# A 21-stage float32 kernel on one core: instruction orders changed in its second and fourth token mixers

## The chip, the cores and the metric

The kernel runs on one core of a Trainium2 chip. The metric is the device time of one execution in microseconds (us); lower is better. The engines are TensorE (PE, with its weight loads as PEld), VectorE (DVE), ScalarE (ACT), GpSimd (POOL) and SyncE (SP), which here issues the weight transfers. Each engine runs its own list of instructions strictly in order and meets the others only through semaphores.

## What is computed

The input is one sequence of 512 tokens with 1024 features, in float32. Two model blocks of two layers each follow one another: norms, token mixers and feed-forward parts. The change touches two of the mixers.

```
def odd_mixer(...):                       # the second mixer
    u, c_q, c_kv, k_rope = split_cols(h @ w_in, ODD_SIZES)
    y_c = s5_group(u, ...)                # linear state space scan, gelu, gate
    y_d = mla_group(c_q, c_kv, k_rope, pos, ...)   # 8 heads, causal by chunks of 64
    return concatenate([y_c, y_d]) @ w_out

# s5_group: A, B are complex, per group of 16 channels
    bu = einsum(u, b_bar); state = associative_scan(a, bu)
    y = real(einsum(state, c)) + d_skip * u
    y = gelu(y); y = y * sigmoid(y @ w_glu + b_glu)

# mla_group
    q = rms_norm(c_q, q_norm) @ w_uq; kv = rms_norm(c_kv, kv_norm) @ w_ukv
    o = softmax(mask((q . k) * scale)) @ v       # q and k each: 64 plain + 32 rotated features

def mlstm_mixer(x, ...):                  # 4 heads, forward and backward in time, chunks of 64
    h = mlstm(q, k, v, gates_forward) + flip(mlstm(flip(...), gates_backward))
    h = normalised over each head's 256 features * norm_g
    return (sigmoid(o) * h) @ w_out
```

## The kernel before, in words

The whole program is one launch of 21 stages. Weights come as 512 KB units of 128 x 1024 numbers, in one fixed order, into a ring of six buffers; SyncE loads unit n once unit n-6 is done on TensorE. Every float32 product is made from three fast products: ScalarE rounds a number to a high part (`hi_to` for the weights, tile WH), VectorE subtracts to get the low part (`lo_to`, tile WL), and TensorE adds high*high, low*high and high*low (lines L310 to L312). The activations have the same two parts, XH and XL. `hi_to(act, n)` and `lo_to(dve, n)` split all units below n, at the place of the program where they stand.

No scheduler orders anything: each mixer has one function per engine (`pe`, `act`, `dve`, `pool`), and the order of calls in it is the order on the engine. An engine that waits on a semaphore holds up all that stands behind it.

**The second mixer** (`od_mixer`; its tiles have names with od_). Units nu to nu+9 are the input projection, nuq to nuq+2 (nu+10 to nu+12) make the queries, nu+13 and nu+14 keys and values, ng and ng+1 the gate, no onward the output. The steps that matter below:

- The normed query and key inputs: VectorE makes `cn(q)` (od_cn, two buffers), ScalarE its high part (od_cqh, od_ckh), VectorE its low part (od_cql, od_ckl), five times.
- B and C of the state space are multiplied by powers of A on VectorE (`turned`, tiles od_bp and od_cp). ScalarE spreads each power into a plane (`plane(d)` writes od_bm, `c_planes(d)` writes od_cmr and od_cmi). TensorE transposes the planes of B into od_bt.
- VectorE rotates queries and keys (od_ab, od_qr, od_kr), with od_cos and od_sin, and builds a table of powers (od_tab).
- Four scans, one per 128 channels: TensorE `states_in(c)` (ps<-od_u,od_bt), VectorE `scan(c)` (od_t, od_vb, then the result in X[c], od_x), TensorE `states_out(c, part)` (ps<-od_u,od_kd, then od_x with od_cmr and od_cmi, and in part 1 od_u,od_skip). ScalarE takes the result (`y(c)`, od_u).
- Eight attention heads. Per head h: TensorE `scores(h)` (ps<-od_k,od_q, into banks 0 to 2), VectorE `maxes(h)`, ScalarE `exps(h)` (od_p), VectorE `weights(h)` (1/sum on a diagonal, od_dgr), TensorE the normalising transposes (ps<-od_dgr,od_p), ScalarE their copies (od_pt), TensorE the product with the values (ps<-od_pt,od_v), ScalarE and VectorE its parts XH and XL. I call the TensorE parts scores, turns and output of a head. Between them stand parts of gelu on ScalarE and VectorE, and on TensorE what the table `beside` names: `states_out` of scans 2 and 3, and the two gate units (ps<-od_gh,WH).

**The mLSTM mixer** (`mlstm_mixer`, tiles with ml_). For each of 4 heads, TensorE `values(h, j)` (ps<-ml_v,ml_e) for four tiles j of 128 tokens, then per tile VectorE `sums` (ml_rc, later ml_h) with ScalarE `backward` (ml_hb) in the middle, then `scales(h)` on VectorE and `normed(h)` on ScalarE; TensorE `turn(h, c)` transposes ml_h, VectorE `gated(k)` multiplies with ml_sig, ScalarE `high(k)` writes XH and VectorE `low(k)` writes XL, for eight k of 128 features. `output(m, ks)` adds the products of k in ks to output tile m; each m has its own unit and bank. `gate(t)` is the o-gate's unit t.

Of the kernel before, what the change touches and what calls it, by code (L numbers as in the profile page):

```python
# [11 lines left out]
P = 128  # L12
# [1867 lines left out]
def od_mixer(nc, b):  # L1880
# [48 lines left out]
    X = [sb("od_x0", [P, 4, 2, NC], at=WORK2 + 8 * KB), sb("od_x1", [P, 4, 2, NC], at=WORK2), sb("od_x2", [P, 4, 2, NC], at=WORK + 80 * KB)]  # L1929
    X += X[1:2]  # L1930
# [38 lines left out]
    GAN = counts("y0 y1 s0 t0 s1 t1 y2 s2 t2 y3 s3 t3 h0 h1 h2 h3 z0 z1 x0 x1 z2 z3 x2 x3")  # L1969
# [27 lines left out]
    def pe(pe, e):  # L1997
# [34 lines left out]
        for g in range(3):  # L2032
            if g == 0:
                pe.wait_ge(s["u_ev"], 3)
            elif g == 1:
                pe.wait_ge(s["u_ev"], 4)
                pe.wait_ge(s["c_ready"], 3)
            else:
                pe.wait_ge(s["q_ev"], 4)
# [11 lines left out]
            elif g == 1:  # L2051
                for a in range(2):
                    pe.wait_ge(s["q_ev"], a + 1)
                    mm(ps[:, a, :], perm[:], QR[:, a, :]).then_inc(s["rot"], 1)
# [84 lines left out]
        pe.wait_ge(s["k_ev"], 21)  # L2139
        states_out(1, 0)  # L2140
        states_out(1, 1)

# [13 lines left out]
        def gate(g):  # L2156
# [4 lines left out]
        beside = {0: lambda: states_out(2, 0), 1: lambda: states_out(2, 1), 2: lambda: states_out(3, 0), 3: lambda: states_out(3, 1),  # L2161
                  5: lambda: gate(0), 6: lambda: gate(1)}
        scores(0)
        for h in range(NH):
            pe.wait_ge(s["comb"], h + 1)
# [10 lines left out]
            if h + 1 < NH:  # L2176
                scores(h + 1)
# [16 lines left out]
    def act(act, own, e):  # L2194
# [49 lines left out]
        hi_to(act, nu + 14)  # L2244
# [107 lines left out]

        y(0)
        y(1)
        exps(0)
        for h in range(NH):
# [18 lines left out]
            if h in (1, 3):  # L2375
                y(2 + h // 2)
# [10 lines left out]
    def dve(dve, own, e, finish, tail):  # L2387
# [96 lines left out]

        own(turned(CP[1], CP[0], AR, XK, C1, C2), "c_ready")
# [23 lines left out]
        def scan(c):  # L2509
# [974 lines left out]
```

## Time and profile before

| | |
|---|---|
| median of 3 runs | 3600.67 us (3599.86 to 3603.81) |
| the profiled execution's own time | 3600.57 us |
| its span | 3598.8 us |
| TensorE busy | 3446.1 us (96%) |
| VectorE busy | 1856.8 us (52%) |
| ScalarE busy | 1309.2 us (36%) |
| transfers | 307.60 MB, mean 85 GB/s |
| mean granted TensorE clock | 0.983 of full |

"Busy" is the time in which an engine had an instruction running. The span runs from the first to the last instruction of the profiled execution. A matmul's start and its length overlap with its neighbours', so the distance from start to start is what one costs in a dense stretch. The granted clock is 1.00 at 2.4 GHz and 0.5 at 1.2 GHz; a mean over a stretch lies between.

### The profile page before, as it was taken

The page shows a single profiled execution, that of the slowest core. Times are in us where ns is not written, and L with a number is a line of the kernel's source. Part 1 is how long each engine was busy: PE and PEld are TensorE (multiplying, and loading weights), DVE is VectorE, ACT ScalarE, POOL GpSimd, SP SyncE. Part 2 cuts the span into 40 slices and gives each one's busy share as a digit, 9 for nine tenths or more (in the row PEclk, how much of TensorE's full clock was granted, in tenths as well). Part 3 has the DMA queues.
Part 4 walks back from the last instruction along what each step waited for, and adds up shares of the span by engine and source line. Part 5 has one row for each costly group of instructions (what it writes and reads, how often), then busy time and mean ns, then how long its engine had stood idle before and what let it go on. Part 6 is the DMA issues. An engine that isn't in the chain of part 4 may idle for free.

```text
span 3598.8 us, 43337 instructions
## 1 busy us (share of the span) xinstructions
PE 3446.1 (96%) x17564; PEld 2834.9 (79%) x17564; DVE 1856.8 (52%) x2971; ACT 1309.2 (36%) x2212; POOL 92.8 (3%) x133
## 2 busy tenths in 40 slices
PE   8989999999978999999999998999999999999998
PEld 7657778888855888888888767888888888788886
DVE  5665775433784544354435346543364336564446
ACT  4442433222454422243223343422242225543233
POOL 0000000000100000000001000100010001010000
PEclk9999999999988999999999999999999999999999
DMA  3102112233300222323232211222322232013244
GB/s 130 53 24 88 59 60 94 100 100 106 92 25 6 77 100 96 104 90 104 100 100 82 101 39 56 82 99 95 105 88 95 98 106 73 30 48 121 96 141 157
DMA packets 92507, 307.60 MB, mean 85 GB/s; under 512 B 16014, under 2 KB 17684, under 8 KB 92308
## 3 DMA queue, kind: packets, MB, share of 16 engines
q1 hardware_dynamic: 89528, 301.31, 25.1%
q10 hardware_dynamic: 2780, 3.51, 0.3%
q8 instruction: 140, 2.29, 0.3%
q14 instruction: 59, 0.48, 0.0%
HBM read 302.69 MB, written 2.10 MB: 85 GB/s over the span
## 4 chain that ended last, share of the span: by engine, by line
PE 81%; DVE 12%; ACT 4%; issue 2%; DMA 0%; SPq 0%; DVEq 0%; POOL 0%; ACTq 0%
PE ps L310 23%; PE ps L311 22%; PE ps L312 22%; PE ps L307 12%; DVE XT L853 1%; DVE WL L298 1%; ACT WH L292 1%; DVE mb_cv L1755 1%; DVE XL L859 1%; PE ps L2738 1%; ACT od_p L2330 0%; DVE R L700 0%; DVE small L2555 0%; DVE mb_e L1816 0%; DMA RAW<-units 0%
## 5 line engine op out<-in xcount | busy, mean ns | idle before, releaser
L310 PE MATMUL ps<-XH,WH 128*128 128x512 f32 (+1 forms) x3200 | 1190.3, 372 | 43.3 <-DVE XL L859 25.9
L311 PE MATMUL ps<-XL,WH 128*128 128x512 f32 (+1 forms) x3200 | 1174.2, 367 | 0.0
L312 PE MATMUL ps<-XH,WL 128*128 128x512 f32 (+1 forms) x3200 | 1173.7, 367 | 0.0
L298 DVE TENSOR_TENSOR WL<-RAW,WH 128x1024 fp32r<-128x1024 f32 x567 | 688.1, 1228 | 320.7 <-ACT WH L292 317.2
L310 PEld LDWEIGHTS ps<-XH,WH 128*128 128x128 f32 x3200 | 608.8, 190 | 153.8 <-DVE XL L859 19.1
L312 PEld LDWEIGHTS ps<-XH,WL 128*128 128x128 f32 x3200 | 609.0, 190 | 97.6
L311 PEld LDWEIGHTS ps<-XL,WH 128*128 128x128 f32 x3200 | 609.6, 190 | 96.1 <-issue 1.7
L292 ACT ACTIVATE WH<-RAW 128x1024 fp32r<-128x1024 f32 x567 | 586.7, 1049 | 138.9 <-DMA RAW<-units 73.6
L310 PE MATMUL ps<-HH,WH 128*128 128x512 f32 (+1 forms) x990 | 362.7, 366 | 0.0
L311 PE MATMUL ps<-HL,WH 128*128 128x512 f32 (+1 forms) x990 | 361.8, 365 | 0.0
L312 PE MATMUL ps<-HH,WL 128*128 128x512 f32 (+1 forms) x990 | 361.7, 365 | 0.0
L589 ACT ACTIVATE HH<-HV 128x512 fp32r<-128x512 f32 x132 | 83.4, 632 | 566.2 <-DVE HV L774 566.2
L771 DVE SCALAR_TENSOR_TENSOR SG<-TH,ps 128x512 f32<-128x512 f32 x132 | 90.7, 687 | 299.1 <-ACT TH L586 298.9
L774 DVE SCALAR_TENSOR_TENSOR HV<-SG,ps 128x512 f32<-128x512 f32 x132 | 90.7, 687 | 296.2 <-PE ps L312 296.0
L700 DVE SCALAR_TENSOR_TENSOR R<-R,ps 128x512 f32<-128x512 f32 (+1 forms) x86 | 51.6, 600 | 362.9 <-PE ps L312 362.2
L490 ACT ACTIVATE SQ<-R 128x512 f32<-128x512 f32 (+1 forms) x89 | 49.1, 551 | 514.2 <-DVE R L700 435.3
L586 ACT ACTIVATE TH<-ps 128x512 f32<-128x512 f32 x132 | 78.7, 596 | 368.5 <-PE ps L312 368.5
L310 PEld LDWEIGHTS ps<-HH,WH 128*128 128x128 f32 x990 | 186.7, 189 | 30.4
L312 PEld LDWEIGHTS ps<-HH,WL 128*128 128x128 f32 x990 | 186.7, 189 | 30.1
L311 PEld LDWEIGHTS ps<-HL,WH 128*128 128x128 f32 x990 | 186.7, 189 | 30.0
L776 DVE TENSOR_TENSOR HL<-HV,HH 128x512 fp32r<-128x512 f32 x132 | 91.5, 693 | 101.5 <-ACT HH L589 101.5
L549 POOL TENSOR_TENSOR XT<-XT,NB 128x256 f32<-128x256 f32 x80 | 74.8, 950 | 2115.0 <-DVE XT L853 2115.0
(607 smaller groups left out, 3467.4 us busy)
## 6 DMA issues: line engine op xcount, KB each, us to landing
RAW<-units SPq DMA_DIRECT2D x567, 512.0 KB, 3.3
XIN<-in_x ACTq DMA_DIRECT2D x2, 1024.0 KB, 6.4
out<-YT SPq DMA_DIRECT2D x8, 256.0 KB, 3.2
GB<-in_ln_g SPq DMA_DIRECT2D x1, 512.0 KB
GB<-in_ln_b SPq DMA_DIRECT2D x1, 512.0 KB
da_pi<-in_positions ACTq DMA_DIRECT2D x1, 256.0 KB, 3.0
mb_pairf<-constants ACTq DMA_DIRECT2D x1, 256.0 KB
wa_dist<-constants ACTq DMA_DIRECT2D x1, 192.0 KB, 2.3
```

Source lines behind the costliest of these rows:

```text
L292: nc.scalar.activation(WH[:, u % RING, :], RAW[:, u % RING, :], ACT.Copy).then_inc(S["wh_ready"], 1)
L298: nc.vector.tensor_tensor(WL[:, u % RING, :], RAW[:, u % RING, :], WH[:, u % RING, :].bitcast(F32), ALU.subtract)\
L307: return nc.tensor.matmul(out, lhsT, rhs, start=start, stop=stop, **kw)
L310: nc.tensor.matmul(out, wh, xh, start=start, stop=False)
L311: nc.tensor.matmul(out, wh, xl, start=False, stop=False)
L312: return nc.tensor.matmul(out, wl, xh, start=False, stop=stop)
L549: nc.gpsimd.tensor_tensor(x, x, NB[:, t // 8, :], ALU.add).then_inc(S["t_ready"], 1)
L586: nc.scalar.activation(TH[:, j % 2, :], ps[:, 2 * (j % 3), :], ACT.Tanh, scale=0.5).then_inc(S["ffn_act"], 1)
L589: nc.scalar.activation(HH[:, j, :], HV[:, j % 2, :], ACT.Copy).then_inc(S["ffn_act"], 1)
L771: own(v.scalar_tensor_tensor(SG[:, j % 2, :], TH[:, j % 2, :], 1.0, ps[:, b, :], ALU.add, ALU.mult))
L774: own(v.scalar_tensor_tensor(HV[:, j % 2, :], SG[:, j % 2, :], e["half"], ps[:, b + 1, :], ALU.mult, ALU.mult), "ffn_dve")
L776: own(v.tensor_tensor(HL[:, j, :], HV[:, j % 2, :], HH[:, j, :].bitcast(F32), ALU.subtract), "ffn_dve")
```

## The change

Nothing is computed in another way; the number of instructions of each kind stays the same, but for one activation more that only sets ScalarE's function table. What moves:

1. Second mixer, input side. ScalarE's copy `u(2)` and the splitting of unit nu+12 no longer stand ahead of the five high parts; `plane(0)` and `plane(1)` move ahead of the copies od_qr, `queries(1)` behind `plane(3)`, and the split of unit nu+13 behind it. VectorE makes the first power of C ahead of those of B, turns the key behind both powers of B, and splits unit nu+13 last. TensorE rotates the queries' source (od_qr,od_perm) ahead of unit nuq+1 and not behind it.
2. Scans. X[2] and X[3] get places of their own, and VectorE's two waits for a free place go (on bt_t 12 and on yc 2).
3. Heads. `scores(h+1)` stands ahead of head h's turns on TensorE, not behind them; `states_out` of scans 1 and 2 stands behind `scores(0)`, ahead of all turns, and scan 3's takes the places beside heads 0 and 1. ScalarE loads the table of exp ahead of `y(0)`, does `exps(0)` ahead of `y(1)`, and `exps(0)` waits for three scans, not four.
4. mLSTM. `values(3, 0)` and `values(3, 1)` stand ahead of gate unit 7, and `values(3, 2)` ahead of the second turn. On VectorE `sums(3, 0)` and `sums(3, 1)` come ahead of the first `low`. The first four output tiles are added up in slices of k (0 to 2, 3, then the turns of head 3, then 4 and 5, then 6 and 7), where before tile 0 and then tile 1 took k 0 to 5, and tiles 2 and 3 came last and whole.

```diff
-    X = [sb("od_x0", [P, 4, 2, NC], at=WORK2 + 8 * KB), sb("od_x1", [P, 4, 2, NC], at=WORK2), sb("od_x2", [P, 4, 2, NC], at=WORK + 80 * KB)]
-    X += X[1:2]
+    X = [sb("od_x0", [P, 4, 2, NC], at=WORK2 + 8 * KB), sb("od_x1", [P, 4, 2, NC], at=WORK2)]
+    X += [sb(f"od_x{c}", [P, 4, 2, NC], at=XH_AT + 4 * c * KB) for c in (2, 3)]
...
             elif g == 1:
+                for a in range(2):
+                    pe.wait_ge(s["q_ev"], a + 1)
+                    mm(ps[:, a, :], perm[:], QR[:, a, :]).then_inc(s["rot"], 1)
                 pe.wait_ge(s["u_ev"], 4)
...
-        pe.wait_ge(s["k_ev"], 21)
-        states_out(1, 0)
-        states_out(1, 1)
...
-        beside = {0: lambda: states_out(2, 0), 1: lambda: states_out(2, 1), 2: lambda: states_out(3, 0), 3: lambda: states_out(3, 1),
-                  5: lambda: gate(0), 6: lambda: gate(1)}
+        beside = {0: lambda: states_out(3, 0), 1: lambda: states_out(3, 1), 5: lambda: gate(0), 6: lambda: gate(1)}
         scores(0)
+        pe.wait_ge(s["k_ev"], 21)
+        for c in (1, 2):
+            states_out(c, 0)
+            states_out(c, 1)
         for h in range(NH):
+            if h + 1 < NH:
+                scores(h + 1)
             pe.wait_ge(s["comb"], h + 1)
...
-            if h + 1 < NH:
-                scores(h + 1)
             if h in beside:
...
-        for t in range(3):
+        for t in range(2):
             u(t)
             hi_to(act, nu + 11 + t)
         for q in range(5):
...
+            if q == 3:
+                u(2)
+        hi_to(act, nu + 13)
...
         def exps(h):
             act.wait_ge(s["max_ready"], h + 1)
-            if h == 0:
-                act.wait_ge(s["x"], 4)
-            if h >= 2:
+            if h < 2:
+                act.wait_ge(s["x"], 3 + h)
+            else:
                 act.wait_ge(s["tr"], 4 * (h - 1))
...
+        A(TMPA[:, 0:1], ones[:, 0:1], ACT.Exp)
         y(0)
+        exps(0)
         y(1)
-        exps(0)
+        y(2)
...
-            elif c == 2:
-                dve.wait_ge(s["bt_t"], 12)
-            elif c == 3:
-                dve.wait_ge(s["yc"], 2)
...
         pe.wait_ge(s["exp"], 56)
-        output(0, range(6))
-        output(1, range(6))
+        for m in range(4):
+            if m == 2:
+                pe.wait_ge(s["ho"], 15)
+            output(m, range(3))
+        for m in range(4):
+            output(m, (3,))
         turn(3, 0, "gy", 5)
         turn(3, 1, "gy", 6)
-        output(0, (6, 7))
-        output(1, (6, 7))
-        outproj_pe(pe, b, e, no, None, XHk, XLk, first=2)
+        for ks in ((4, 5), (6, 7)):
+            for m in range(4):
+                output(m, ks)
+        outproj_pe(pe, b, e, no, None, XHk, XLk, first=4)
```

ScalarE, input side of the second mixer, of before and then of the change (od_u is a copy of a projected tile, WH<-RAW the split of a weight unit, od_bm a plane of B):

```order
L2206 ACTIVATE od_u<-ps 128x512
L292 ACTIVATE WH<-RAW 128x1024
L2239 ACTIVATE od_cqh<-od_cn 128x512 x3
L2239 ACTIVATE od_ckh<-od_cn 128x512 x2
L2242 DMA od_q<-constants 4x8x512
L2206 ACTIVATE od_u<-ps 128x512
L292 ACTIVATE WH<-RAW 128x1024
L2283 ACTIVATE od_qr<-ps 128x512 x2
L2211 ACTIVATE od_bm<-od_bp_168,small 128x2x16x16 x2
```

```order
L2237 ACTIVATE od_cqh<-od_cn 128x512 x3
L2237 ACTIVATE od_ckh<-od_cn 128x512
L2204 ACTIVATE od_u<-ps 128x512
L2237 ACTIVATE od_ckh<-od_cn 128x512
L292 ACTIVATE WH<-RAW 128x1024
L2243 DMA od_q<-constants 4x8x512
L2204 ACTIVATE od_u<-ps 128x512
L2209 ACTIVATE od_bm<-od_bp_168,small 128x2x16x16 x2
L2209 ACTIVATE od_bm<-od_bp_169,small 128x2x16x16 x2
L2285 ACTIVATE od_qr<-ps 128x512 x2
```

The first row of before (the copy of the third tile, which waits for TensorE) and the split behind it now stand inside and behind the high parts, and two planes stand ahead of od_qr.

TensorE, heads 4 and 5 of the second mixer, of before and then of the change (od_dgr,od_p are a head's turns, od_k,od_q the next head's scores, od_pt,od_v its output):

```order
L307 MATMUL ps<-od_dgr,od_p_208 128x128 x10
L307 MATMUL ps<-od_k,od_q 128x512
L307 MATMUL ps<-od_k,od_q 128x128
L307 MATMUL ps<-od_k,od_q 128x384
L307 MATMUL ps<-od_k,od_q 128x256
L307 MATMUL ps<-od_pt_210,od_v 64x512
L307 MATMUL ps<-od_pt_210,od_v 64x384
L307 MATMUL ps<-od_pt_210,od_v 64x256
L307 MATMUL ps<-od_pt_210,od_v 64x128
L307 MATMUL ps<-od_dgr,od_p_209 128x128 x10
```

```order
L307 MATMUL ps<-od_k,od_q 128x512
L307 MATMUL ps<-od_k,od_q 128x128
L307 MATMUL ps<-od_k,od_q 128x384
L307 MATMUL ps<-od_k,od_q 128x256
L307 MATMUL ps<-od_dgr,od_p_209 128x128 x10
L307 MATMUL ps<-od_pt_211,od_v 64x512
L307 MATMUL ps<-od_pt_211,od_v 64x384
L307 MATMUL ps<-od_pt_211,od_v 64x256
L307 MATMUL ps<-od_pt_211,od_v 64x128
```

Scores of the next head have moved from behind a head's turns to ahead of them.

ScalarE, end of the mLSTM mixer, of before and then of the change (ml_hb is `backward`, ml_sig `gate(7)`, XH<-ml_sig `high`, ml_h `normed`):

```order
L3196 ACTIVATE ml_h<-ml_h,ml_tm 128x256 x4
L3167 ACTIVATE ml_sig<-ps 128x512
L292 ACTIVATE WH<-RAW 128x1024
L3201 ACTIVATE XH<-ml_sig,ml_gain 128x512
L3191 ACTIVATE ml_hb<-ps,ml_rc 128x256
L3201 ACTIVATE XH<-ml_sig,ml_gain 128x512
L3191 ACTIVATE ml_hb<-ps,ml_rc 128x256
L3201 ACTIVATE XH<-ml_sig,ml_gain 128x512
```

```order
L3200 ACTIVATE ml_h<-ml_h,ml_tm 128x256 x4
L292 ACTIVATE WH<-RAW 128x1024
L3195 ACTIVATE ml_hb<-ps,ml_rc 128x256 x2
L3170 ACTIVATE ml_sig<-ps 128x512
L3205 ACTIVATE XH<-ml_sig,ml_gain 128x512 x2
L3195 ACTIVATE ml_hb<-ps,ml_rc 128x256
L3205 ACTIVATE XH<-ml_sig,ml_gain 128x512
```

The first two `backward` of head 3 have moved ahead of the gate's activation and of the first two high parts.

## Rows read from the trace of the kernel before

**Rows 1.** Windows: stretch, us and count busy by engine, granted clock, DMA share, GB/s.
```profile
1020.00:1185.00 165.00, 125.55 (x948) 88.77 (x947) 92.67 (x165) 73.84 (x178) 1.80 (x1) 0.87 0.04 14
2166.00:2222.00 56.00, 46.00 (x183) 36.80 (x182) 31.25 (x82) 17.79 (x29) 0.00 (x0) 0.88 0.12 38
...
1146.75:1152.34 5.59, 5.59 (x26) 1.00 0.02 3
1165.17:1172.95 7.78, 7.78 (x24) 0.71 0.00 0
```

**Rows 2.** Timeline (start, length, [idle before <-releaser]), ScalarE then VectorE, input side.
```profile
975.75 0.60 ACT L2206 ACTIVATE od_u<-ps 128x512 f32<-128x512 f32 x1 [6.84 <-PE ps L312]
...
977.92 0.69 DVE L2462 TENSOR_TENSOR od_cql<-od_cn,od_cqh 128x512 fp32r<-128x512 f32 x1 [6.13 <-ACT od_cqh L2239]
```

**Rows 3.** Timeline, TensorE: third query unit starts; VectorE: the table starts.
```profile
993.15 0.79 PE L310 MATMUL ps<-od_cqh,WH 128*128 128x512 f32 x1
...
1001.29 0.07 DVE L2490 MEMSET od_tab<- 128x16 f32 x1
```

**Rows 4.** Timeline, TensorE: `states_in(1)` of the second scan.
```profile
1024.93 1.28 PE L307 MATMUL ps<-od_u,od_bt 32*128 32x128 f32 x16 [4.51 <-DVE od_t L2517]
```

**Rows 5.** Timeline, VectorE: results of scans 2 and 3.
```profile
1055.06 0.69 DVE L2532 TENSOR_TENSOR od_x<-od_vb,od_t 128x512 f32<-128x512 f32 x1 [1.45 <-PE ps L307]
...
1069.16 0.69 DVE L2532 TENSOR_TENSOR od_x<-od_vb,od_t 128x512 f32<-128x512 f32 x1 [4.03 <-PE ps L307]
```

**Rows 6.** Timeline, TensorE: `states_out(1)`, `scores(0)`, first turns.
```profile
1063.56 2.57 PE L307 MATMUL ps<-od_u,od_kd 128*128 128x512 f32 x8
...
1068.89 2.32 PE L307 MATMUL ps<-od_k,od_q 100*128 100x512 f32 x8
1077.78 1.44 PE L307 MATMUL ps<-od_dgr,od_p 128*128 128x128 f32 x5 [6.56 <-DVE od_dgr L2565]
```

**Rows 7.** Timeline, TensorE: turns and output of one head, and the next turns.
```profile
1126.01 2.90 PE L307 MATMUL ps<-od_dgr,od_p 128*128 128x128 f32 x20 [0.86 <-DVE od_dgr L2565]
...
1131.00 2.37 PE L307 MATMUL ps<-od_pt,od_v 128*64 128x512 f32 x8
1136.22 3.35 PE L307 MATMUL ps<-od_dgr,od_p 128*128 128x128 f32 x14 [2.85 <-DVE od_dgr L2565]
1142.36 1.01 PE L307 MATMUL ps<-od_dgr,od_p 128*128 128x128 f32 x3 [2.78 <-ACT od_pt L2361]
```

**Rows 8.** Timeline, VectorE, same head: maxima, last gelu step.
```profile
1131.11 1.68 DVE L2555 TENSOR_REDUCE small<-ps 128x1 f32<-128x512 f32 x4 [3.15 <-PE ps L307]
...
1138.91 0.69 DVE L2541 SCALAR_TENSOR_TENSOR od_u<-od_gw,od_u 128x512 f32<-128x512 f32 x1
```

**Rows 9.** Timeline, ScalarE: the gate's four high parts; TensorE: gate unit 1, last output.
```profile
1139.64 2.19 ACT L2380 ACTIVATE od_gh<-od_u 128x512 fp32r<-128x512 f32 x4 [0.93 <-DVE od_u L2541]
...
1165.17 0.79 PE L310 MATMUL ps<-od_gh,WH 128*128 128x512 f32 x1 [5.32 <-ACT od_y L2347]
...
1178.96 2.34 PE L307 MATMUL ps<-od_pt,od_v 128*64 128x512 f32 x8 [0.51 <-ACT od_pt L2361]
```

**Rows 10.** Timeline, TensorE, end of mLSTM: values of head 3 and output products.
```profile
2171.79 4.49 PE L307 MATMUL ps<-ml_v,ml_e 128*128 128x257 f32 x20
...
2179.36 6.29 PE L307 MATMUL ps<-ml_v,ml_e 128*128 128x257 f32 x20 [2.20 <-DVE ml_h L3302]
...
2194.37 0.80 PE L310 MATMUL ps<-XH,WH 128*128 128x512 f32 x1 [4.78 <-DVE XL L3318]
...
2202.78 1.04 PE L3056 MATMUL ps<-ident,ml_h 128*128 128x128 f32 x8
2205.95 0.47 PE L310 MATMUL ps<-XH,WH 128*128 128x512 f32 x1 [2.13 <-DVE XL L3318]
```

**Rows 11.** Timeline, VectorE: third XL part; output tile 3 taken.
```profile
2183.19 0.75 DVE L3318 SCALAR_TENSOR_TENSOR XL<-ml_sig,ml_gain,XH 128x512 fp32r<-128x512 f32 x1
...
2221.51 0.69 DVE L700 SCALAR_TENSOR_TENSOR R<-R,ps 128x512 f32<-128x512 f32 x1 [0.30 <-PE ps L312]
```

More of the change, by code:

```diff
@@ L1968, in od_mixer @@
     GLN = counts("w0 g0 w1 g1 w2 g2 w3 g3 l0 l1 l2 l3 m0 m1 x0 x1 m2 m3 x2 x3")
-    GAN = counts("y0 y1 s0 t0 s1 t1 y2 s2 t2 y3 s3 t3 h0 h1 h2 h3 z0 z1 x0 x1 z2 z3 x2 x3")
+    GAN = counts("y0 y1 y2 s0 t0 s1 t1 y3 s2 t2 s3 t3 h0 h1 h2 h3 z0 z1 x0 x1 z2 z3 x2 x3")
     N_ROW, N_IN = 5, 12
@@ L2050, in pe @@
                 last.then_inc(s["rot"], 1)
[L2051 to L2054, printed above, removed]
         for n in range(8):
@@ L2243, in act @@
         u(3)
-        hi_to(act, nu + 14)
         def queries(g):
@@ L2279, in keys @@
                 A(K[0:64, h, :], ps[0:64, PB[h % 4], :], ACT.Copy).then_inc(s["k_ev"], 1)
+        plane(0)
+        plane(1)
         act.wait_ge(S["unit_done"], done_at(e["nuq"]))
@@ L2283, in act @@
             A(QR[:, a, :], ps[:, a, :], ACT.Copy).then_inc(s["q_ev"], 1)
-        plane(0)
         act.wait_ge(s["rot"], 2)
@@ L2287, in act @@
         A(SIN[:], ps[:, 3, :], ACT.Copy).then_inc(s["q_ev"], 1)
-        plane(1)
-        queries(1)
         plane(2)
         plane(3)
+        queries(1)
+        hi_to(act, nu + 14)
         queries(2)
@@ L2374, in act @@
                 tanh(min(h, 3))
-            if h in (1, 3):
-                y(2 + h // 2)
+            if h == 1:
+                y(3)
             elif h == 4:
@@ L2468, in dve @@
             own(v.tensor_tensor(CP[0][:, i], CP[0][:, i], both[:, :, 1, :], ALU.add), "c_ready")
-        lo_to(dve, nu + 14)
+        own(turned(CP[1], CP[0], AR, XK, C1, C2), "c_ready")
         for d in range(2):
@@ L2472, in dve @@
             own(turned(BP[d], BP[1 - d], AR, XK, B1, B2), "b_ready")
-            if d == 0:
+            if d == 1:
                 dve.wait_ge(s["q_ev"], 4)
@@ L2483, in dve @@
             own(v.tensor_tensor(QR[:, a, :], AB[:, 0, :], AB[:, 1, :], ALU.add), "rope_done")
-        own(turned(CP[1], CP[0], AR, XK, C1, C2), "c_ready")
+        lo_to(dve, nu + 14)
         dve.wait_ge(s["ws"], 1)
@@ L3101, in pe @@
             values(2, j)
-        gate(7, 1, "gy", 4)
         values(3, 0)
         values(3, 1)
+        gate(7, 1, "gy", 4)
         turn(2, 0, "ev", 23)
+        values(3, 2)
         turn(2, 1, "ev", 24)
-        values(3, 2)
         values(3, 3)
@@ L3167, in gate @@
             A(SIG[:, t, :], ps[:, t % 2, :], ACT.Tanh, scale=0.5).then_inc(s["ev"], 1)
-            hi_to(act, ns + t + 5)
+            if t < 7:
+                hi_to(act, ns + t + 5)
         def weights(h, d):
@@ L3224, in act @@
             normed(h)
-            gate(2 * h + 3)
-        for j in range(TT):
-            high(j)
-            backward(3, j)
+            if h < 2:
+                gate(2 * h + 3)
+        hi_to(act, ns + 12)
+        backward(3, 0)
+        backward(3, 1)
+        gate(7)
+        high(0)
+        high(1)
+        backward(3, 2)
+        high(2)
+        backward(3, 3)
+        high(3)
+        hi_to(act, ns + 13)
         high(4)
@@ L3340, in dve @@
             scales(h)
-            lo_to(dve, ns + 2 * h + 8)
+            if h < 2:
+                lo_to(dve, ns + 2 * h + 8)
+        sums(3, 0)
+        sums(3, 1)
+        lo_to(dve, ns + 12)
         low(0)
-        sums(3, 0)
         low(1)
-        sums(3, 1)
+        gated(4)
+        sums(3, 2)
         low(2)
-        gated(4)
         gated(5)
-        sums(3, 2)
+        sums(3, 3)
         low(3)
-        sums(3, 3)
         scales(3)
+        lo_to(dve, ns + 13)
         low(4)
```

## The prediction

> **What bounds the kernel now.** TensorE is busy for 96% of the span, so I look for the stretches where it isn't, and the two that the change touches are among them. From 1020 to 1185 us (scans and heads of the second mixer) it is busy for 125.6 of 165 us at a mean granted clock of 0.87; from 2166 to 2222 us (end of mLSTM) for 46.0 of 56 us at 0.88 [rows 1]. So 39.4 and 10.0 us are idle there, and part of the rest runs at 1.2 GHz. What can be won is idle time of TensorE and low clock behind it. Nothing else in the program moves.
>
> I then read who ends each idle time. In the scans it is VectorE (4.51 us before `states_in(1)` [rows 4]), which is itself busy nearly without a gap there, so the scans go as fast as VectorE comes to them. In the heads it is the chain scores, maxima, exp, weights, turns: 6.56 us before the first turns [rows 6], 2.85 before those of head 5, and 2.78 more in the middle of them, because ScalarE copies the gate's inputs first [rows 7, 9]. Gate unit 1 waits 5.32 us for ScalarE [rows 9]. In mLSTM TensorE waits 2.20, 4.78 and 2.13 us for VectorE, and 0.9 us in one more place [rows 10].
>
> **Input side.** VectorE idles 6.13 us between the first two normed tiles and their low parts. ScalarE, which owes it the high parts, stands at `u(2)` until TensorE ends a unit at 975.7 [rows 2]. With the high parts ahead, VectorE goes on at once: a gain of 6.1 at most. Three waits take part of it back. `plane(0)` writes over XH, so it can't start before TensorE has left the projection (0.8 us lost, as I count it); the sine copy waits for TensorE's replication behind the first query unit (0.9); and the split of unit nu+13 stands behind `queries(1)`, thus behind the query unit that now ends near 993.7, about where the next one started before [rows 3] (1.8). I carry them as estimates: net 2.8, bounds 0 and 6.1. The table then starts at 998.5 instead of 1001.3 [rows 3]. TensorE itself gains nothing up to here: it is dense and only changes the order of its units, and the transposes of B still wait for ScalarE.
>
> **Scans.** All four scans move up by 2.8, and the wait of 4.51 us shrinks to 1.7. Removing the two waits for a place takes 1.45 and 4.03 us off VectorE [rows 5], so the last scan ends 2.8 + 1.45 + 4.03 = 8.3 us earlier, at about 1062.2 instead of 1070.5. TensorE ends `states_out(0)` 2.8 us earlier, at 1060.8, and goes straight to `scores(0)` (2.3 us), which end at 1063.1: maxima from there, exp and weights as before, 6.5 us from the end of scores to the first turns less 1.3 us for the function table that is loaded ahead; so the weights are ready near 1068.4.
>
> Meanwhile TensorE has `states_out(1)` (5.3 us, from 1063.56 to 1068.89 [rows 6]), `states_out(2)` (the same kind, 5.6) and `scores(1)` (2.3) to do, back to back, and starts the first turns near 1075.8. Before, it started them at 1077.8 with the latter two still to come. The gain at this point is 2.0 + 5.6 + 2.3 = 9.9 us. What hides the softmax chain of head 0 is those 13 us of work; without it 5 us would be back.
>
> **Heads.** A head costs TensorE 2.7 (turns) + 2.3 (scores) + 2.3 (output) = 7.3 us [rows 6, 7], if nothing waits. In the new order the chain from scores to weights has turns, output and the next scores beside it. It isn't TensorE that limits a head then but VectorE's round: from its maxima to the end of the last gelu step took 8.5 us, waits for exp included [rows 8], and the next maxima stand behind it. So I take 8.5 us a head for the heads without extra work, against 10.2 us from turns to turns before (1126.0 to 1136.2 [rows 7]). Heads 0 and 1 carry `states_out(3)` and go at TensorE's pace, 11.2 and 9.7.
>
> Two waits stay. Head 5's turns still need ScalarE, which has the gate's four copies (2.19 us [rows 9]) ahead; I keep 2.4 us, and 1.0 for low clock behind it, where before there were 2.85 + 2.78. Gate unit 1 still needs ScalarE's two activations, now behind turns and exp alone: 4.0 us instead of 5.32 after 2.3 of scores. The unit behind it then takes 7.8 us again instead of the 5.6 of a dense one [rows 1].
>
> So: first turns at 1075.8; 11.2 + 9.7 + 3 x 8.5 later, at 1122.2, those of head 5; with 2.7 + 2.4 + 1.0 for them and 5.6 for gate unit 0, that is done at 1133.9; output, scores and turns (2.3 + 2.3 + 2.7) and 4.0 of waiting bring gate unit 1 to 1145.2; 7.8 for it, 2.3 for an output, 2.7 for the last turns, 0.5 for ScalarE's copies and 2.3 for the last output end at 1160.8. I add 1.2 for hand-overs that dense rows don't show: 1162.0, where before it was 1178.96 + 2.34 = 1181.3 [rows 9]. The second mixer gains 19.3 us, 9.9 before the heads begin and 9.4 in them. Bounds of the heads' part: 0 (each head stays at its old length) and 14 (TensorE's 7.3 us a head, nothing added).
>
> **mLSTM.** Old waits: 10.0 us [rows 1]. What low clock cost on top: ten values' products took 4.49 us dense and 6.29 behind a wait (1.8); 24 output products took 8.4 us, from 2194.37 to 2202.78, where a dense unit of 24 takes 5.6 less the overlap at its end, 5.45 (3.0); the 60 from 2205.95 to 2221.4 took 15.5 instead of 13.6 (1.9) [rows 1, 10, 11]. Together 16.7.
>
> In the new order `values(3, 0..1)` need only results of head 2 and the gate unit covers head 3's first sums, so the 2.20 goes. Sixteen steps of k stand ahead of the last turns instead of twelve, and none of them needs XL 4 or 5, which made TensorE wait 4.78. Behind the turns stand eight steps that need no new XL (5.4 us), while VectorE needs about 3 for the last two; the 2.13 goes. One wait comes: the third XL part is now behind two more sums and a weight split on VectorE. It was ready at 2183.9 [rows 11], I expect 2185.4, and TensorE is there at 2183.7. That is 1.8 us, and 1.7 for low clock behind it. Gain 16.7 - 3.5 = 13.2 (bounds 8 and 16.7); following TensorE step by step I get tile 3 done at 2208.7 instead of 2221.4, 12.7. I take 12.9.
>
> **Sum.** 19.3 + 12.9 = 32.2 off 3600.57 us, the profiled execution's own time, which is the median of the runs shown (3600.67) within 0.1. That gives 3568.4.
>
> **Rule against row.** In mLSTM four accumulating tiles are now open at once, and no tile's k runs through. The rows show low clock only behind waits of 2 us and more, and weights and inputs of all four tiles are on chip, so I expect one wait and not one per slice. A page of the Trainium skill speaks against such a loop: "TensorE: Matmul & The Clock Gate", "Why this matters for your kernels", asks for thin matmuls to loop K-contiguous, else the clock oscillates with each tile. By the rows the projection costs 21.8 us for 96 products plus the 3.5 above; by that page's rule it would be the second rival's 12 us more.
>
> **Rivals.** (1) *The heads don't shorten.* VectorE's round holds a serial wait for exp, and if copies and exp queue on ScalarE behind each other a head stays at 10.2. For it: ScalarE has some 7.5 us of work in a head. Against it: the maxima of the next head now fall inside the turns. It takes away up to 9.4: 3578.
>
> (2) *The sliced output runs at low clock.* 24 products at mostly low clock took 8.4 us instead of 5.45 [rows 10]; for 96 that is 12 us more, and four tiles ending within 4 us leave VectorE behind with their sums (up to 2 more). The gain of mLSTM is gone: 3582. For it: each slice may wait for its XL part. Against: the parts come every 3 us or so while a slice lasts 2.7 to 8.
>
> (3) *Slower.* TensorE falls to 1.2 GHz for most of the heads: scores ahead of turns make it wait in each head for exp of the head before (its banks are read by it), at a fixed place, 2 us each time. Those waits are 16 us, and the other 16 that are needed to be slower than before come once 30 of the heads' 75 us of products run at the low clock (8.4 against 5.45 above is 1.54 times as long). With all 75 us of them it would be 3568.4 + 16 + 40 = 3624; I put it at 3610. Against it: its stretch is at 0.87 to 0.88 even with all the waits of today.
>
> (4) *Nothing comes of it*, because the time that VectorE wins is given back at the next meeting with TensorE. The scans speak against it, where VectorE's own end decides. 3599.
>
> **Chances.** My forecast 0.68, with its own range 3561 to 3575; (1) 0.13; (2) 0.09; (1) and (2) partly together, near 3590, 0.03; (4) 0.03; (3) 0.04. The range of 8 in 10 goes from 3560 to 3583: below it only a head at TensorE's own pace and no new wait in mLSTM. A measurement of this kernel can tell about 0.2% (7 us) from no change, so faster 0.93, same 0.03, slower 0.04.
>
> **What the next profile shows if I am right.** VectorE has no 6 us idle before its first od_cql, and its table starts near 998.5. The idle time before `states_in(1)` is under 2 us, before the first turns it is none, and turns follow each other by about 8.5 us in heads 2 to 4. One wait of 4 us before gate unit 1 stays. The last output of the heads is done about 19 us earlier. In mLSTM one wait of about 2 us stands in the output products, before the third k. I am wrong if a new wait on od_p or od_k,od_q appears in every head, if the granted clock from 1020 on falls under 0.85, or if the projection of mLSTM shows waits at each slice.

## The result, and the profile after

The change takes the median from 3601.02 us (3599.86 to 3603.81, 4 runs) to 3566.58 us (3561.93 to 3568.85, 4 runs): a ratio of 0.9902, 95% interval 0.9884 to 0.9919, 34.4 us less. Medians leave out two executions at a much lower clock, one of *ml2* (5708.86 us at 0.56) and one of the kernel before beside it (4326.06 us at 0.75). I had predicted 3568. The profiled execution of the changed kernel took 3568.85 us, its span is 3567.0 us, TensorE is busy for 97% of it at a mean clock of 0.985.

Two executions can't be compared by their absolute times alone. VectorE's instruction `R<-R,ps` takes each output tile of a stage and is the same in both kernels, so it serves as a milestone: one ahead of the second mixer, the first behind it, one ahead of mLSTM, one behind it. Timeline of VectorE, kernel before:

```profile
914.24 0.42 DVE L700 SCALAR_TENSOR_TENSOR R<-R,ps 128x256 f32<-128x256 f32 x1
1188.43 0.69 DVE L700 SCALAR_TENSOR_TENSOR R<-R,ps 128x512 f32<-128x512 f32 x1 [1.39 <-PE ps L312]
1961.10 0.42 DVE L700 SCALAR_TENSOR_TENSOR R<-R,ps 128x256 f32<-128x256 f32 x1
2250.11 0.42 DVE L700 SCALAR_TENSOR_TENSOR R<-R,ps 128x256 f32<-128x256 f32 x1
```

The same four of the changed kernel:

```profile
919.21 0.42 DVE L700 SCALAR_TENSOR_TENSOR R<-R,ps 128x256 f32<-128x256 f32 x1
1171.68 0.69 DVE L700 SCALAR_TENSOR_TENSOR R<-R,ps 128x512 f32<-128x512 f32 x1 [1.36 <-PE ps L312]
1944.38 0.42 DVE L700 SCALAR_TENSOR_TENSOR R<-R,ps 128x256 f32<-128x256 f32 x1
2220.02 0.42 DVE L700 SCALAR_TENSOR_TENSOR R<-R,ps 128x256 f32<-128x256 f32 x1
```

The second mixer goes from 274.19 to 252.47 us (1188.43 - 914.24, 1171.68 - 919.21), mLSTM from 289.01 to 275.64 us: 21.7 and 13.4 us less, 35.1 together. What lies between the second and the third milestone differs by less than 0.1 us. But this execution came 4.97 us late to the first milestone, in stages that both kernels share; so I add 5.0 to times of before when I compare within the second mixer, and take 16.7 off within mLSTM. Below, "the milestones say" means such a difference against the kernel before.

Windows of the changed kernel (stretch, us and count busy by engine, granted clock, DMA share, GB/s). The first two are the work of [rows 1], ended where the same work ends:

```profile
1025.00:1168.25 143.25, 121.07 (x948) 86.41 (x947) 89.91 (x159) 73.34 (x179) 1.80 (x1) 0.90 0.05 16
2149.30:2191.90 42.60, 40.04 (x185) 32.88 (x184) 27.59 (x78) 16.13 (x27) 0.00 (x0) 1.00 0.13 38
1059.17:1067.30 8.13, 8.12 (x75) 5.28 (x75) 7.89 (x15) 1.46 (x2) 0.00 (x0) 0.62 0.01 2
1082.29:1126.13 43.84, 41.75 (x256) 27.35 (x255) 26.75 (x51) 30.45 (x78) 0.00 (x0) 1.00 0.00 1
2169.24:2178.91 9.67, 9.67 (x42) 7.95 (x43) 7.76 (x24) 5.34 (x9) 0.00 (x0) 1.00 0.00 1
```

TensorE's idle time in the second mixer's stretch falls from 39.4 to 22.2 us, in mLSTM's from 10.0 to 2.6. Heads 0 to 4 (fourth row) run at 2.4 GHz throughout; `states_out(0)` (third row) starts behind four waits (2.37, 0.47, 0.50 and 1.68 us) and runs mostly at 1.2 GHz. The last row is mLSTM's projection from its one wait to the last turns.

VectorE's timeline, input side of the changed kernel (start, length, [idle before <-releaser]):

```profile
976.79 0.69 DVE L2465 TENSOR_TENSOR od_cql<-od_cn,od_cqh 128x512 fp32r<-128x512 f32 x1
...
988.97 0.69 DVE L2398 TENSOR_TENSOR od_b<-od_bp,od_small 128x512 f32<-128x512 f32 x1 [0.92 <-ACT od_bm L2209]
...
994.10 0.68 DVE L2478 TENSOR_TENSOR od_ab<-od_krs,od_cos 32x512 f32<-32x512 f32 x1 [0.92 <-ACT od_sin L2288]
...
1002.27 1.23 DVE L298 TENSOR_TENSOR WL<-RAW,WH 128x1024 fp32r<-128x1024 f32 x1 [1.81 <-ACT WH L292]
1003.46 0.07 DVE L2492 MEMSET od_tab<- 128x16 f32 x1
```

The 6.13 us of [rows 2] are gone and three waits of 0.92, 0.92 and 1.81 us have come. The table of powers starts at 1003.46. TensorE's timeline, second scan and heads:

```profile
1027.11 1.17 PE L307 MATMUL ps<-od_u,od_bt 32*128 32x128 f32 x16 [1.75 <-DVE od_t L2519]
...
1082.29 0.27 PE L307 MATMUL ps<-od_dgr,od_p 128*128 128x128 f32 x1
...
1110.13 2.79 PE L307 MATMUL ps<-od_dgr,od_p 128*128 128x128 f32 x20
1113.39 2.34 PE L307 MATMUL ps<-od_pt,od_v 128*64 128x512 f32 x8 [0.46 <-ACT od_pt L2364]
1116.08 2.43 PE L307 MATMUL ps<-od_k,od_q 100*128 100x512 f32 x8 [0.35 <-ACT od_p L2331]
1118.34 2.79 PE L307 MATMUL ps<-od_dgr,od_p 128*128 128x128 f32 x20
...
1126.13 1.73 PE L307 MATMUL ps<-od_dgr,od_p 128*128 128x128 f32 x14
1130.67 1.65 PE L307 MATMUL ps<-od_dgr,od_p 128*128 128x128 f32 x6 [2.82 <-ACT od_pt L2364]
...
1149.28 0.50 PE L310 MATMUL ps<-od_gh,WH 128*128 128x512 f32 x1 [3.56 <-ACT od_y L2348]
```

No wait is left before the first turns, a head without extra work takes 8.2 us from turns to turns (1110.13 to 1118.34), and two waits above 1 us remain in the heads. mLSTM has one wait in the output products, for the third XL part (TensorE):

```profile
2169.24 0.51 PE L310 MATMUL ps<-XH,WH 128*128 128x512 f32 x1 [2.50 <-DVE XL L3331]
2178.91 1.04 PE L3054 MATMUL ps<-ident,ml_h 128*128 128x128 f32 x8
```

### The profile page after: what moved, and what is told of

It is laid out like the page before. It is cut to its first block, busy times and chain, and to the rows that moved or that the text cites. A ratio compares the mean times of both kernels' runs of the same rounds, so it can differ in the third digit from the quotient of the medians.

```text
span 3567.0 us, 43351 instructions
## 1 busy us (share of the span) xinstructions
PE 3443.3 (97%) x17564; PEld 2836.7 (80%) x17564; DVE 1856.5 (52%) x2971; ACT 1309.8 (37%) x2213; POOL 93.0 (3%) x133
## 4 chain that ended last, share of the span: by engine, by line
PE 83%; DVE 11%; ACT 4%; issue 2%; DMA 0%; SPq 0%; DVEq 0%; POOL 0%; ACTq 0%
PE ps L310 23%; PE ps L311 23%; PE ps L312 23%; PE ps L307 13%; DVE XT L853 1%; DVE WL L298 1%; ACT WH L292 1%; DVE mb_cv L1755 1%; DVE XL L859 1%; PE ps L2736 1%; DVE R L700 1%; DVE S L709 0%; ACT od_p L2331 0%; PE ps L1096 0%; ACT SQ L490 0%
```

## The experiments

Each kernel was timed against the kernel before on the same chip. That kernel's own median lay between 3600.5 and 3603.9 us from one experiment to the next, so two medians of different experiments can differ by some 3 us for that reason alone, and I compare such kernels by their ratios. Milestones come from one profiled execution of each. How far a milestone difference can be trusted: the second mixer, with the same code as in the changed kernel, took 252.02 to 252.70 us in four traces.

**1 and 2. Each half alone** (no further edit: the diff's hunks of one mixer).

> The kernel before with the mLSTM part of the change alone. By my step of the sum it is 12.9 us faster than before (3588); read off the two traces, 13.4 us (3587.6). If the gain of mLSTM hung on the second mixer being shorter too (weights that arrive late, or drift between executions taken for a gain), it would be under 8 us.

Measured: 3590.28 us, ratio 0.9963 (0.9950 to 0.9976), 13.6 us less by the medians. The milestones say 11.9 in mLSTM and 0.2 in the second mixer, where nothing was changed.

> The kernel before with the part of the change in the second mixer alone. Predicted 19.3 us faster (3581.7); read off the two traces, 21.7 us (3579.3). The heads at their old length would leave 10 us of it (3591).

Measured: 3579.17 us (3573.03 to 3585.99), ratio 0.9934 (0.9916 to 0.9952). The milestones say 22.2 us in the second mixer, and 0.7 more in mLSTM, where nothing was changed. The two halves make 33.6 us by the milestones, the whole change 35.1: they add up but for 1.5 us, which mLSTM gains only in the whole (13.4 and not 11.9).

**3. The place of the scores** in the changed kernel:

```diff
         for h in range(NH):
-            if h + 1 < NH:
-                scores(h + 1)
             pe.wait_ge(s["comb"], h + 1)
...
                 last.then_inc(s["tr"], 1)
+            if h + 1 < NH:
+                scores(h + 1)
```

> The changed kernel with the next head's scores behind a head's turns again. My theory (the softmax chain of the next head has to run beside turns and output, not beside the output alone): from the end of scores to the next turns it takes 5.2 us with the table loaded ahead, and 2.4 us of output lie beside it, so heads 2, 3 and 4 wait 2.5 to 3 us each again and the time is 8 to 12 us longer than the changed kernel (3575 to 3579). Rival: the heads got shorter because states_out moved out from between them, and the place of the scores is worth 2 us or less (3569).

Measured: 3591.59 us, ratio 0.9956 (0.9940 to 0.9973), 25.0 us more than the changed kernel by the medians, 19.4 by the ratios; I had expected 8 to 12. The five runs fall into two groups (3579.77 and 3581.62; 3591.59, 3592.42 and 3592.61), and the trace is of one in the upper group. What the lower two did no trace shows; they too are 13 us and more above the changed kernel's median. By the milestones of the trace the second mixer is 0.7 us shorter than before, no more: with this one move undone, the others are worth next to nothing there. That isn't to say that the move alone is worth 21 us. In the kernel before, with the same order, parts of `states_out` stood beside heads 0 to 3 and the turns of heads 1 to 4 waited 0, 0.86, 0 and 0.86 us at their start; the change takes them away from heads 2 and 3. No run has the scores moved and `states_out` left. TensorE's timeline, heads 2 and 3 of this kernel and the next turns:

```profile
1103.15 1.83 PE L307 MATMUL ps<-od_dgr,od_p 128*128 128x128 f32 x14 [0.86 <-DVE od_dgr L2563]
...
1116.94 2.44 PE L307 MATMUL ps<-od_dgr,od_p 128*128 128x128 f32 x14 [2.92 <-DVE od_dgr L2563]
1119.97 1.65 PE L307 MATMUL ps<-od_dgr,od_p 128*128 128x128 f32 x6 [0.58 <-ACT od_pt L2364]
1121.41 4.00 PE L307 MATMUL ps<-od_k,od_q 100*128 100x512 f32 x8
1125.35 2.37 PE L307 MATMUL ps<-od_pt,od_v 128*64 128x512 f32 x8
1130.64 0.60 PE L307 MATMUL ps<-od_dgr,od_p 128*128 128x128 f32 x3 [2.92 <-DVE od_dgr L2563]
```

Its windows, all heads and then those scores alone:

```profile
1081.64:1187.40 105.76, 83.65 (x404) 56.18 (x402) 43.33 (x80) 48.33 (x121) 0.00 (x0) 0.87 0.03 10
1121.41:1125.35 3.94, 3.94 (x9) 1.97 (x9) 0.00 (x0) 0.48 (x2) 0.00 (x0) 0.57 0.00 0
```

The same window of the changed kernel, from the first turns to the last output:

```profile
1082.29:1164.93 82.64, 73.14 (x396) 50.01 (x394) 43.33 (x80) 47.52 (x120) 0.00 (x0) 0.96 0.04 13
```

The wait is as I sized it (2.92 us before the turns of heads 3 and 4). What I left out is the clock behind it: the scores take 4.00 us and not 2.43, and a head 13.7 us, not 8.2. Of the 23.1 us between the two windows 12.6 are idle time of TensorE (22.1 against 9.5) and 10.5 are busy time. Of these, 2.2 are `scores(1)`, eight products that stand ahead of the first turns in the changed kernel and behind them here (x404 against x396); 8.3 are the same products running longer.

**4. Whole tiles in mLSTM**, the output order of before in the changed kernel:

```diff
-        for m in range(4):
-            if m == 2:
-                pe.wait_ge(s["ho"], 15)
-            output(m, range(3))
-        for m in range(4):
-            output(m, (3,))
+        output(0, range(6))
+        output(1, range(6))
         turn(3, 0, "gy", 5)
         turn(3, 1, "gy", 6)
-        for ks in ((4, 5), (6, 7)):
-            for m in range(4):
-                output(m, ks)
-        outproj_pe(pe, b, e, no, None, XHk, XLk, first=4)
+        output(0, (6, 7))
+        output(1, (6, 7))
+        outproj_pe(pe, b, e, no, None, XHk, XLk, first=2)
```

> The changed kernel with mLSTM's output tiles added up as before: tile 0 and 1 over k 0 to 5, the turns, k 6 and 7 of both, then tiles 2 and 3 whole. My theory: the slices pay because TensorE has 16 steps that need no late XL part; whole tiles meet k 3, 4 and 5 before VectorE has made them, which adds waits of about 3.2 and 3.8 us and 2 to 3 us of low clock: 8 to 10 us longer than the changed kernel (3575 to 3577), most of mLSTM's 13.4 us. Rival (the rule of k running through in one tile): the slices cost clock, and whole tiles are as fast or faster (3566 or less).

Measured: 3579.60 us, ratio 0.9936 (0.9920 to 0.9953), which is 12.2 us more than the changed kernel by the ratios, where I had expected 8 to 10; the milestones leave 1.2 us of mLSTM's 13.4. Its timeline on TensorE has four waits for XL instead of one:

```profile
2166.18 0.50 PE L310 MATMUL ps<-XH,WH 128*128 128x512 f32 x1 [2.51 <-DVE XL L3326]
2170.09 0.79 PE L310 MATMUL ps<-XH,WH 128*128 128x512 f32 x1 [2.94 <-DVE XL L3326]
2174.59 0.79 PE L310 MATMUL ps<-XH,WH 128*128 128x512 f32 x1 [2.85 <-DVE XL L3326]
2181.92 1.04 PE L3054 MATMUL ps<-ident,ml_h 128*128 128x128 f32 x8
2185.10 0.73 PE L310 MATMUL ps<-XH,WH 128*128 128x512 f32 x1 [2.13 <-DVE XL L3326]
```

The slices are worth 12.2 us: 7.9 of waits (the last three), and 4.3 in which TensorE is busy longer (44.3 us against 40.0 over the same work, at a clock of 0.88 against 1.00).

**5. The old input side** (the diff's hunks of the input side undone on TensorE, ScalarE and VectorE).

> The changed kernel with the input side of the second mixer (all three engines) in its old order. By my step VectorE starts its table 2.8 us later and the scans, which VectorE sets, carry that through to the last head: 2.8 us longer than the changed kernel (3569.4). Rivals: the whole of the removed idle time counts, 6.1 us (3572.7); or TensorE's own work from the first states_out on hides it, 0 (3566.6).

Measured: 3568.55 us (3567.93 to 3572.42), ratio 0.9904 (0.9889 to 0.9919), 2.0 us more than the changed kernel by the medians, 0.7 by the ratios: too little for either to tell from nothing, so the traces have to decide. VectorE's timeline:

```profile
978.08 0.69 DVE L2463 TENSOR_TENSOR od_cql<-od_cn,od_cqh 128x512 fp32r<-128x512 f32 x1 [6.13 <-ACT od_cqh L2238]
...
1001.45 0.07 DVE L2491 MEMSET od_tab<- 128x16 f32 x1
```

This execution is 0.17 us late at the first milestone and the changed one 4.97: the table starts at 1001.28 against 998.49 on the clock of before, 2.8 us apart. The whole mixer is 3.5 us longer, and the other 0.7 are clock, to within 0.2 us. `states_out(0)` also starts 2.8 us later, but takes 7.09 us (1057.18 to 1064.27) and not 8.13; the heads take 84.52 us and not 82.64, with the same 9.5 us idle. Window of these heads:

```profile
1079.26:1163.78 84.52, 75.01 (x396) 51.12 (x395) 43.34 (x80) 47.56 (x121) 0.00 (x0) 0.94 0.04 13
```

**6. No table ahead** (without the line `A(TMPA[:, 0:1], ones[:, 0:1], ACT.Exp)`).

> The changed kernel without the activation that loads the function table ahead. 13 us of TensorE's work lie beside the softmax chain of head 0, whose weights are ready 7.5 us before TensorE asks for them, so I expect no change (within 1 us of the changed kernel). Rival: the load of 1.28 us stands on the path and the time is 1.3 us longer.

Measured: 3567.93 us, ratio 0.9900 (0.9885 to 0.9915); the milestones say 0.0 us. The load is hidden either way: the weights of head 0 are ready 7.4 us before TensorE asks for them in the changed kernel (1074.85 against 1082.29).

**7. A place for the last scan**, in the kernel before, run twice:

```diff
-    X += X[1:2]
+    X += [sb("od_x3", [P, 4, 2, NC], at=XH_AT + 12 * KB)]
...
-            elif c == 3:
-                dve.wait_ge(s["yc"], 2)
```

> The kernel before with a place of its own for the result of the last scan alone, so that VectorE's wait of 4.03 us for it is gone; all orders as before. I expect the last scan to end 4 us earlier and the kernel to gain 0 to 1 us, because the maxima of head 0 then wait for scores(0), which stand behind states_out(1) on TensorE: the places pay only with the new order of scores(0). Rival: the removed wait is a gain by itself, 4.0 us (3597).

> The kernel x3_place once more, unchanged, because its runs were 5.8 us faster than before while its trace shows only 0.4 us at the edit and 3.0 us in mLSTM, which it does not touch (the same waits there, 0.92 of granted clock and not 0.89). If those 3 us are a matter of the execution, this trace shows anything between before and 3 us less in mLSTM, again 0.4 us in the second mixer, and the ratio lies nearer to 1 (0.9985 to 1.0000). If the edit is worth 4 us, the ratio stays at 0.9989 or less and the mixer's part shows it.

Measured: 3596.33 us (10 runs), ratio 0.9984 (0.9974 to 0.9993), then 3599.71 us (11 runs), ratio 0.9993 (0.9984 to 1.0002). Both traces say 0.4 us in the second mixer: the removed 4.03 us of VectorE are given back at its next meeting with TensorE, as long as `scores(0)` stand where they did. VectorE's timeline of the first run, the maxima of head 0:

```profile
1072.13 1.68 DVE L2553 TENSOR_REDUCE small<-ps 128x1 f32<-128x512 f32 x4 [4.97 <-PE ps L307]
```

And both say 3.0 us less in mLSTM, which the edit doesn't touch. If that were a matter of the execution, the second trace could have shown anything between 0 and 3; it shows the same. The two ratios agree only within their intervals, and the second can't be told from no change. More on it at the end.

**8 to 11. What is left.** *gates*: ScalarE takes the result of gate unit 0 ahead of its copies of head 6, and the gate's high parts and unit 0 come later (part of the edit, on ScalarE; VectorE's low parts and TensorE's unit 0 move with it):

```diff
+            if h == 6:
+                gate(0)
+                gate(1)
             if h >= 2:
                 act.wait_ge(s["o_ready"], h - 1)
...
+            if h == 5:
+                act.wait_ge(s["gl"], GLN["g3"])
+                for c in range(4):
+                    A(GH[:, c, :], U[:, c, :], ACT.Copy, scale=0.5).then_inc(s["ga"], 1)
             if h + 1 < NH:
                 exps(h + 1)
```

> The changed kernel with two waits of the heads attacked. ScalarE takes the result of gate unit 0 ahead of its copies of head 6, so that gate unit 1 has its banks in time; the gate's four high parts stand behind the copies of head 5, and gate unit 0 stands behind the output of head 5, each of its steps waiting for its own low part. The waits of 2.82 and 3.56 us go, with about 1.8 us of low clock behind the second: 6 to 8 us shorter than the changed kernel (3559 to 3561). Rival: the waits only move, since ScalarE then takes exp of head 6 later and scores of head 7 wait for it: within 2 us.

Measured: 3559.89 us (3553.41 to 3562.23), ratio 0.9875 (0.9860 to 0.9889); the milestones say 10.3 us on top of the change, the ratios 9.7, and I had expected 6 to 8. TensorE's waits from 1060 us to the projection (us in total, times, longest):

```profile
PE ps L307 <- ACT od_pt L2373: 2.8, 6, 0.5
PE ps L310 <- DVE XL L2556: 0.7, 1, 0.7
PE ps L307 <- ACT od_p L2337: 0.4, 1, 0.4
```

The waits of 2.82 and 3.56 us are gone and none has come. From the first turns (1076.59) to the end of the last output (1150.24) it takes 73.65 us, TensorE busy for 69.99 of them at full clock, against 82.64 and 73.14 at 0.96: 5.8 us less idle and 3.2 less for the same products, where I had counted 1.8 for clock. The other 1.3 us were won ahead of the heads, where this kernel is unchanged: `states_out(0)` starts behind the same waits but takes 6.82 us and not 8.13 (TensorE's timeline):

```profile
1054.78 4.06 PE L307 MATMUL ps<-od_u,od_kd 128*128 128x512 f32 x8 [1.67 <-ACT od_kd L2326]
...
1061.60 2.32 PE L307 MATMUL ps<-od_k,od_q 100*128 100x512 f32 x8
```

That is clock, and I can't credit it to the edit: in experiment 4, whose second mixer is the changed kernel's, the same part takes 6.83 us as well, and its mixer is no shorter for it (252.70 us).

*chunks* (part of the edit; each `states_out(c)` also waits for its own part of od_kd alone):

```diff
+        own_chunk(0)
+        own_chunk(1)
         states_in(3)
-        for c in range(4):
-            own_chunk(c)
-        pe.wait_ge(s["bt_done"], 24)
+        own_chunk(2)
+        own_chunk(3)
```

> The changed kernel with TensorE's four small products for od_kd moved: two ahead of the last states_in, where TensorE waits 2.37 us, and states_out(c) waiting for its own part of od_kd only. TensorE then starts states_out(0) near 3 us earlier and at full clock, and from there to the turns of head 0 it is dense: 4 to 5.7 us shorter than the changed kernel (3561 to 3562.6). Rival: VectorE's scans set the end all the same (the maxima of head 0 stand behind the last scan), and it is within 1 us.

Measured: 3560.03 us, ratio 0.9885 (0.9869 to 0.9901); the milestones say 6.4 us, more than the 4 to 5.7 that I expected: `states_out(0)` starts 4.9 us earlier, not 3. Its window where `states_out(0)` to the first turns lie, TensorE busy for 34.92 of 35 us at full clock:

```profile
1050.00:1085.00 35.00, 34.92 (x401) 23.47 (x394) 25.00 (x47) 14.83 (x42) 0.00 (x0) 1.00 0.02 7
```

*ml2* puts high parts 0 to 3 and low parts 0 to 2 of mLSTM ahead of the last two sums, and the gating of head 2 behind head 3's scales.

> The changed kernel with mLSTM's last part in another order on ScalarE and VectorE: high and low parts 0 to 2 ahead of the last two sums, the gating of head 2 behind the scales of head 3. The wait of 2.50 us before the third k and about 1.7 us of low clock behind it go; the last turns may wait up to 1 us for the normed head 3: 3 to 4.2 us shorter than the changed kernel (3562.4 to 3563.6). Rival: the wait moves whole to the last turns, within 1 us.

Measured: 3563.36 us, ratio 0.9896 (0.9875 to 0.9918); the milestones say 2.6 us, the wait of 2.50 alone, and not the 3 to 4.2 that I expected: behind it there was no low clock to win back (1.00 in the projection's window above).

> The three edits (gates, chunks and the other order of mLSTM) together. If each works at its own place they add up: 13 to 18 us shorter than the changed kernel (3549 to 3554). Rival: the edits of the second mixer overlap, since an earlier start of the heads meets the same round of VectorE, and the sum stays under 10 us.

Measured: 3547.03 us (3544.65 to 3551.17), ratio 0.9851 (0.9835 to 0.9867), 19.6 us under the changed kernel and 53 under before, a little more than the 13 to 18 that I expected. The milestones say 16.5 + 2.6 us, against 10.3 + 6.4 + 2.6 of the three alone: they add up.

## Why the prediction was right, step by step

**Input side: right in each term.** Waits 0.8, 0.9 and 1.8 expected, 0.92, 0.92 and 1.81 found; net 2.8, and experiment 5 gives 2.8 at the table and at the start of `states_out(0)`.

**Scans: right on VectorE, 1.5 us short on TensorE.** `states_in(1)` waits 1.75 us (1.7 expected), and the last scan ends at 1062.2 on the clock of before, as predicted. The first turns start at 1082.29, which is 1077.3 on that clock, and not 1075.8. `states_out(0)` starts 2.4 us earlier than before, not 2.8, and I had moved it at its old length, 6.99 us; it takes 8.13, at a clock of 0.62. The gain before the heads is thus 8.4 us, not 9.9. My reading that the rows show low clock only behind waits of 2 us and more didn't hold either: at this very place in the kernel before, behind waits of 0.84, 0.51 and 1.67 us, the eight products below take 4.23 us, and those of the next scan, without a wait, 2.57 [rows 6] (TensorE's timeline, kernel before):

```profile
1056.57 4.23 PE L307 MATMUL ps<-od_u,od_kd 128*128 128x512 f32 x8 [1.67 <-ACT od_kd L2319]
```

The prediction's sum also has a slip: from 1060.8 its terms 2.3, 5.3, 5.6 and 2.3 lead to 1076.3 and not to 1075.8. It did no harm, because dense they take 15.0 us and not 15.5. Experiment 7 adds that the last scan's own place does not pay as long as `scores(0)` stand where they did.

**Heads: right that they shorten, wrong in what limits them.** From first turns to the end of the last output I had 86.2 us and the trace has 82.64. I let VectorE's round of 8.5 us set the pace. It doesn't: turns follow each other by 7.8, 8.2 and 7.8 us in heads 2 to 4, which is TensorE's 7.3 and a wait of 0.46 for ScalarE's last copy. The 8.5 of [rows 8] held a gelu step that head 3 doesn't have, so a long round is made good by the next: VectorE's round takes 9.35 us in head 2 and 7.21 in head 3, and all that reaches TensorE is the wait of 0.35 us for exp. That is 1.7 us; heads 0 and 1 took 0.9 less than I said, and what follows gate unit 1's wait 1.2. The waits of 2.4 and 4.0 us that I kept measured 2.82 and 3.56. With 1.5 lost before the heads, 3.6 won in them and 0.3 at the projection's first wait, the second mixer gained 21.7 and not 19.3.

**mLSTM: the size right, with errors that cancel.** 13.4 in this trace, 11.9 where it stands alone, 12.9 predicted, from 16.7 of old cost less 3.5 of new (13.2) and a count that gave 12.7. The third XL part came 2.0 us later than before, not 1.5, and TensorE waited 2.50, not 1.8; but behind it the clock stayed at 1.00, where I had charged 1.7 us. So the new cost is 2.6 us and not 3.5. The old one was not 16.7 but 16.0: 10.0 idle, and 6.0 and not 6.7 of low clock (TensorE is busy for 46.00 us before and 40.04 after over the same work). That the two errors, 0.9 and 0.7, meet is luck; in experiment 1 the low clock that I had charged is there, 1.6 us of it.

**Sum.** 35.1 by the milestones against 32.2; the medians say 34.4. The profiled execution's own 31.7 is 5.0 less because of its late start, and 1.7 more because the stages behind mLSTM, which no edit touches, took that much less in it. So the time came out near 3568 with a second mixer that gained 2.4 us more than predicted.

**The rivals.** (1) Heads that don't shorten: excluded here, but experiment 3 shows how near it lies, one call away. (2) Slices at low clock: excluded, the projection runs at 1.00 from its one wait to the turns (2169.24 to 2178.91 us, window above). The Trainium skill's page "TensorE: Matmul & The Clock Gate" ("Why this matters for your kernels") asks for K-contiguous loops in thin matmuls; experiment 4 went the other way by 12.2 us, because the inputs of a whole tile were late and those of a slice were not. The page's own case has TensorE wait for a transfer at each K-tile; here there was one wait of 2.50 us in the whole projection. (3) Scores that make TensorE wait for exp of the head before: there is such a wait, 0.35 us, in one head. Its second part, low clock through the heads, did not come (0.96 from the first turns to the last output); experiment 3 shows some of it, 0.87 there, behind waits of 2.9 us. (4) Nothing comes of it: nearly true of one edit alone (0.4 us, experiment 7), not of the whole.

## What to carry to other kernels

Put the next item's first step ahead of this item's last, so that a chain over three engines has a full step of TensorE beside it: taking that one move back cost 21 of 35 us in the trace. Count a repeated wait at more than its length: in experiment 3 12.6 us of idle time came with 8.3 us of low clock, though one wait of 2.50 us in mLSTM came with none. Compare two executions from milestones that both share, stage by stage. An edit that frees an engine can gain nothing until what it meets next is moved too: 4.03 us freed on VectorE were worth 0.4 here.

## What I had not expected of the hardware

The time up to the first milestone, in stages that no kernel here changes, differs between the 14 traces by up to 8.1 us (914.24 to 922.31), while the stages between the second and the third milestone repeat within 0.05 us (772.66 to 772.71). Behind mLSTM the time differs again, by up to 3.8 us (1344.9 to 1348.7). And the runs of one kernel can lie further apart than that first stretch explains: experiment 2's cover 13 us, experiment 3's too, and each has one trace, of one of the longest. So a milestone difference tells what that one execution did.

The same waits don't always cost the same clock. `states_out(0)` above is one case, 8.13 and 6.82 us behind the same waits. mLSTM's waits are 7.8 us in three and 2.4 in two both before and in experiment 7, yet the windows over the same work differ. Kernel before:

```profile
2160.00:2225.00 65.00, 54.78 (x220) 43.77 (x219) 37.55 (x101) 20.80 (x34) 0.00 (x0) 0.89 0.13 41
```

The second run of experiment 7:

```profile
2161.62:2226.62 65.00, 54.75 (x239) 44.35 (x238) 38.67 (x103) 21.09 (x35) 0.00 (x0) 0.92 0.13 42
```

And behind the wait for the third XL part, 2.50 us in the changed kernel and 2.48 in experiment 1, the way to the turns took 9.67 us in the one and 11.25 in the other (TensorE's timeline of experiment 1):

```profile
2190.15 0.50 PE L310 MATMUL ps<-XH,WH 128*128 128x512 f32 x1 [2.48 <-DVE XL L3333]
2201.40 0.82 PE L3056 MATMUL ps<-ident,ml_h 128*128 128x128 f32 x6
```

The two traces of one kernel agree (2.98 and 2.96 us less than before), and so do the five with the changed mLSTM and a second mixer at its new length or near it (13.36 to 13.41). The two whose second mixer is as long as before gain less in the same code: 11.87 in experiment 1 and 11.73 in experiment 3, where the second mixer has most of its edits but not the gain. So it looks like a property of the kernel's timing and not of chance; what decides it stays open.
